# A convolution module on one core: gated tiles left in PSUM, tap products moved last, squares summed by TensorE

## What is computed

```
def conformer_conv_module(u, w_pw1, b_pw1, dw_w, dw_b, ln_g, ln_b, w_pw2, b_pw2):
    h = u @ w_pw1 + b_pw1
    a, g = jnp.split(h, 2, axis=-1)
    h = a * jax.nn.sigmoid(g)
    h = causal_depthwise_conv(h, dw_w, dw_b)      # 31 taps per channel
    h = jax.nn.silu(layernorm(h, ln_g, ln_b))     # mean and variance over the 1024 channels
    return h @ w_pw2 + b_pw2
```

## Time and profile before

| | |
|---|---|
| time, median of 3 runs | 2702.26 us (2699.66 to 2703.58) |
| the profiled execution, its own time | 2701.71 us |
| its span in the profile | 2699.7 us |
| TensorE busy, share of the span | 95% |
| VectorE, ScalarE, GpSimd busy | 50%, 34%, 39% |
| TensorE's mean granted clock | 0.968 of full |
| 40 slices, the 15th to 17th: TensorE busy tenths | 9, 6, 9 |

### The profile page before, as it was taken

The page is one execution under the profiler, slowest core; times in us unless marked ns, Lnnn a source line. Parts: engine busy times, 40 slices in busy tenths (PEclk is TensorE's granted clock), DMA queues, the critical chain, the costliest instruction groups (busy, mean ns, idle before and its releaser), DMA issues.

```text
span 2699.7 us, 29217 instructions
## 1 busy us (share of the span) xinstructions
PE 2570.2 (95%) x11811; PEld 2096.0 (78%) x11811; DVE 1359.8 (50%) x2012; ACT 927.1 (34%) x1539; POOL 1057.5 (39%) x486
## 2 busy tenths in 40 slices
PE   8989999899999996999999899998999999999999
PEld 6778878788888775878888688886766667788887
DVE  6665566565554788474444652224255554422222
ACT  3434334222223284322222232223355543222221
POOL 4333343544444311544444444443222224554443
PEclk9989999899999997999999899999999999999999
DMA  4111221355542200354432232232111112233232
GB/s 147 47 55 62 64 76 50 123 173 164 164 155 95 77 32 8 102 172 161 159 118 94 72 99 97 94 101 78 55 55 47 40 54 86 86 95 100 94 101 86
DMA packets 70982, 252.55 MB, mean 94 GB/s; under 512 B 8000, under 2 KB 8512, under 8 KB 70848
## 3 DMA queue, kind: packets, MB, share of 16 engines
q1 hardware_dynamic: 58752, 210.27, 23.9%
q10 hardware_dynamic: 12096, 40.42, 4.5%
HBM read 248.56 MB, written 2.10 MB: 93 GB/s over the span
## 4 chain that ended last, share of the span: by engine, by line
PE 82%; DVE 13%; ACT 3%; issue 1%; ACTq 0%; DVEq 0%
PE ps L485 24%; PE ps L487 23%; PE ps L486 23%; DVE arena L1359 3%; DVE tmpm L1359 2%; PE ps L501 2%; PE ps L562 1%; PE ps L628 1%; DVE XL L1368 1%; PE ps L702 1%; PE ps L703 1%; PE ps L704 1%; DVE arena L1630 1%; PE ps L524 1%; PE ps L531 1%
## 5 line engine op out<-in xcount | busy, mean ns | idle before, releaser
L2043 POOL TENSOR_TENSOR WL<-raw,WH 128x1024 fp32r<-128x1024 f32 x391 | 953.4, 2442 | 1264.6 <-ACT WH L871 1257.8
L485 PE MATMUL ps<-XH,WH 128*128 128x512 f32 x3160 | 1253.8, 397 | 50.9 <-DVE XL L1359 12.9
L486 PE MATMUL ps<-XL,WH 128*128 128x512 f32 x3160 | 1239.6, 392 | 0.0
L487 PE MATMUL ps<-XH,WL 128*128 128x512 f32 x3160 | 1239.4, 392 | 0.0
L485 PEld LDWEIGHTS ps<-XH,WH 128*128 128x128 f32 x3160 | 600.4, 190 | 187.2 <-issue 24.9
L487 PEld LDWEIGHTS ps<-XH,WL 128*128 128x128 f32 x3160 | 599.0, 190 | 127.3
L486 PEld LDWEIGHTS ps<-XL,WH 128*128 128x128 f32 x3160 | 600.1, 190 | 124.2 <-issue 1.8
L871 ACT ACTIVATE WH<-raw 128x1024 fp32r<-128x1024 f32 x306 | 321.6, 1056 | 682.0 <-PE ps L487 500.2
L1359 DVE SCALAR_TENSOR_TENSOR arena<-arena,ps 128x512 f32<-128x512 f32 x88 | 60.4, 687 | 329.9 <-ACT arena L1072 296.3
L2041 POOL CAST WH<-raw 128x1024 fp32r<-128x1024 f32 x85 | 95.3, 1121 | 279.3 <-PE ps L487 256.1
L1359 DVE SCALAR_TENSOR_TENSOR tmpm<-arena,tmpm 128x512 f32<-128x512 f32 x44 | 83.4, 1895 | 152.1 <-ACT arena L1067 152.1
(11 more groups left out here) (246 smaller groups left out, 2047.4 us busy)
## 6 DMA issues: line engine op xcount, KB each, us to landing
raw<-in_w SPq DMA_DIRECT2D x394, 512.0 KB, 3.7
arena<-in_w_mod ACTq DMA_DIRECT2D x72, 512.0 KB, 4.0
o_out<-h SPq DMA_DIRECT2D x8, 256.0 KB, 2.0
h<-in_x ACTq DMA_DIRECT2D x4, 256.0 KB, 6.9
h<-in_x SPq DMA_DIRECT2D x4, 256.0 KB, 7.3
raw<-in_w SPq DMA_DIRECT2D x2, 256.0 KB, 4.2
arena<-in_c ACTq DMA_DIRECT2D x1, 512.0 KB, 5.4
vec<-in_vec ACTq DMA_DIRECT2D x1, 295.5 KB, 10.3
```

Source lines behind the costliest of these rows:

```text
L485: e.matmul(b, wh, XH[:, x, :], start=i == 0, stop=False)
L486: e.matmul(b, wh, XL[:, x, :], start=False, stop=False)
L487: p = e.matmul(b, wl, XH[:, x, :], start=False, stop=i == len(slots) - 1)
L2043: e.tensor_tensor(lo, x, hi.bitcast(F32), SUB).then_inc(*did(("split", c)))
```

## The change

Six things, all in `conformer()`:

1. Tiles 0 to 2 (`IN_PSUM = 3`) are gated in place in their PSUM bank (5, 6 and 7, `XB`; all the rest of the projection uses the five banks `CB`), and their chains read PSUM. The bank is free when the chain is done. Since no zero padding lies ahead of a tile in PSUM, a step of tap k works on the last 512 - (30 - k) columns only; the steps of the other tiles are cut in the same way.
2. The affine half of the sigmoid moves from VectorE to ScalarE (a second activation behind the tanh).
3. All projections stand ahead of all tap products on TensorE; the numbers of chain steps between the gate instructions change (`more`).
4. The last taps are split, `taps(7, 0, 8)`, the spread of the half mean, `taps(7, 8)`.
5. The squares are summed by TensorE, tile by tile, in PSUM; GpSimd's `squares()` is gone.
6. `centre` and the multiplication by 1/sd read the spread values from PSUM; ScalarE writes its tanh to PSUM; the affine form is made by VectorE (a tensor-scalar into `tmp`).

```
+        IN_PSUM = 3
...
+                CB, XB = (0, 1, 2, 3, 4), (5, 6, 7)
                 for i in range(2, NT):
-                    linear([("pw", 0, 8 + i)], [pw1(8 + i)], X8, x_at, ALL)
-                    linear([("pw", 0, i)], [pw1(i)], X8, x_at, ALL)
-                    if i >= 6:
-                        taps(i - 3)
-                taps(5)
-                taps(6)
-                b = bank(("mean", 0), ALL)
+                    linear([("pw", 0, 8 + i)], [pw1(8 + i)], X8, x_at, CB)
+                    linear([("pw", 0, i)], [pw1(i)], X8, x_at, XB if i < IN_PSUM else CB)
+                for i in range(3, 7):
+                    taps(i)
+                b = bank(("mean", 0), XB)
...
-                taps(7)
+                taps(7, 0, 8)
                 w.wait_ge(*at("mean", 0))
-                spread(("mw", 0), small("mean", 0), ALL)
...
+                spread(("mw", 0), small("mean", 0), XB)
+                taps(7, 8)
+                mean, var = bank(("mean", 1), XB), bank(("var", 0), XB)
+                for i in range(NT):
+                    if i >= 4:
+                        w.wait_ge(*at("cen", i))
+                        p = token_sums(mean, cv[i], one, i == 4, i == NT - 1)
...
+                    w.wait_ge(*at("csq", i))
+                    token_sums(var, tmp[i % 4], one, i == 0, i == NT - 1).then_inc(
...
-                    A(g, g, ACT.Tanh, bias=cols(hb, i), scale=0.5).then_inc(*did(("cgt", i)))
+                    A(g, g, ACT.Tanh, bias=cols(hb, i), scale=0.5).then_inc(*did())
+                    w.wait_ge(s_act, did.n)
+                    A(g, g, ACT.Identity, bias=half_col, scale=0.5).then_inc(*did(("cgt", i)))
...
+                    x = ps("pw", 0, i) if i < IN_PSUM else xp[i][:, K - 1:K - 1 + T]
...
+                        late = K - 1 - k
+                        d = STT(cv[i][:, late:T], x[:, 0:T - late], V("dw_w", 8 * k + i), cv[i][:, late:T], MUL, ADD)
...
-                    if i > 1:
-                        more(10)
+                    more(2 if i > 1 else 0)
...
-                    TS(g, g, 0.5, 0.5, MUL, ADD).then_inc(*did())
...
+                    more((0, 7, 9, 1, 1, 1, 1, 1)[i])
                     if TAPS[i]:
...
+                        more(8)
...
-                    TT(cv[i], cv[i], rs[1], SUB).then_inc(*did(("cen", i)))
+                    TT(cv[i], cv[i], ps("mw", 0), SUB).then_inc(*did(("cen", i), *((("free", "mw", 0),) if i == NT - 1 else ())))
...
-                        TT(cv[i], cv[i], r, MUL).then_inc(*did(("cn", i)))
+                        TT(cv[i], cv[i], ps("vw", 0), MUL).then_inc(*did(("cn", i), *((("free", "vw", 0),) if i == NT - 1 else ())))
+                        own()
+                        w.wait_ge(*at("sum", "var", 0))
+                        TS(zi[i % 4], cv[i], cols(hg, i), cols(hlb, i), MUL, ADD).then_inc(*did(("zi", i)))
...
-            def squares():
```

More of the change, by code:

```diff
@@ L476, in linear @@
             def linear(keys, tiles, slots, ready, of, between=None):
-                bs = [bank(k, of) for k in keys]
+                bs = [bank(k, o) for k, o in zip(keys, of if isinstance(of[0], tuple) else [of] * len(keys))]
                 for i, x in enumerate(slots):
@@ L691, in pw1, with taps @@
                     return column("cv_w_pw1", 0, c)
-                def taps(i):
-                    b = bank(("tap", i), ALL)
+                def taps(i, k0=0, k1=K):
+                    if k0 == 0:
+                        tap_bank[i] = bank(("tap", i), CB)
+                    b = tap_bank[i]
                     a0 = by_pe.index(i) * W
                     w.wait_ge(*at("xp_lo", i))
-                    for k in range(TAPS[i]):
+                    for k in range(k0, min(k1, TAPS[i])):
                         n = sum(TAPS[:i]) + k
@@ L722, in conformer @@
                 p.then_inc(*did(("sum", "mean", 0)))
-                taps(7)
+                taps(7, 0, 8)
                 w.wait_ge(*at("mean", 0))
-                spread(("mw", 0), small("mean", 0), ALL)
[L726 to L735, removed]
+                spread(("mw", 0), small("mean", 0), XB)
[5 more added lines that the diff above has]
+                        p = token_sums(mean, cv[i], one, i == 4, i == NT - 1)
+                        if i == NT - 1:
+                            p.then_inc(*did(("sum", "mean", 1)))
+                    w.wait_ge(*at("csq", i))
+                    token_sums(var, tmp[i % 4], one, i == 0, i == NT - 1).then_inc(
+                        *did(("vs", i), *((("sum", "var", 0),) if i == NT - 1 else ())))
                 w.wait_ge(*at("mean", 1))
-                spread(("mw", 1), small("mean", 1), ALL)
+                spread(("mw", 1), small("mean", 1), CB)
                 w.wait_ge(*at("var"))
-                spread(("vw", 0), small("var"), ALL)
+                for n in range(3):
+                    bank(("t", n), XB)
+                spread(("vw", 0), small("var"), CB)
                 def y_at(i):
@@ L1159, in conformer, with diagonals @@
                 widen(rs[0], ("s2", "w"), ("r", "s2"))
-                def taps(i):
-                    for k in range(TAPS[i]):
+                def diagonals():
+                    for i, k in tap_list:
                         n = sum(TAPS[:i]) + k
@@ L1169, in taps @@
                         A(gl, ident, ACT.Copy, scale=wlo[:, 8 * k + i:8 * k + i + 1]).then_inc(*did(("diag", i, k)))
+                        yield
+                diagonal = diagonals()
                 for i in range(NT):
                     round_weights("pw", 0, i)
-                    if i >= 6:
-                        taps(i - 3)
                     g = cgl[i % 3]
@@ L1183, in conformer @@
                         A(fh[:, a0:a0 + K - 1 + T], xp[i][:, 0:K - 1 + T], ACT.Copy).then_inc(*did(("xp_hi", i)))
[L1184 to L1187, removed]
+                    if i == 5:
+                        for _ in diags:
+                            next(diagonal)
+                for _ in diagonal:
+                    pass
                 sqrt_table()
@@ L1204, in conformer @@
                     if i < NT:
-                        t = tmp[i % 2]
                         w.wait_ge(*at("cn", i))
[L1207 to L1213, removed]
+                        if i >= 3:
+                            w.wait_ge(*at("cy", i - 3))
+                        A(ps("t", i % 3), cv[i], ACT.Tanh, bias=cols(hlb, i), scale=cols(hg, i)).then_inc(*did(("cyt", i)))
                     if i:
@@ L1785, in conformer @@
                 TS(hg, Vs("ln_g", 0, 8), 0.5, None, MUL)
-                TS(hlb, Vs("ln_b", 0, 8), 0.5, None, MUL).then_inc(*did(("hb",)))
-                for a in xp:
-                    e.memset(a[:, 0:K - 1], 0.0).then_inc(*did())
+                TS(hlb, Vs("ln_b", 0, 8), 0.5, None, MUL)
+                e.memset(half_col, 0.5).then_inc(*did(("hb",)))
+                for i in by_pe:
+                    e.memset(xp[i][:, 0:K - 1], 0.0).then_inc(*did())
                 own()
@@ L1800, in chain @@
                         w.wait_ge(s_dve, n)
-                        d = STT(cv[i], xp[i][:, k:k + T], V("dw_w", 8 * k + i), cv[i], MUL, ADD)
-                        d.then_inc(*did(*((("cv", i),) if k == K - 2 and not TAPS[i] else ())))
+                        late = K - 1 - k
+                        d = STT(cv[i][:, late:T], x[:, 0:T - late], V("dw_w", 8 * k + i), cv[i][:, late:T], MUL, ADD)
+                        d.then_inc(*did(*((("cv", i), ("free", "pw", 0, i)) if k == K - 2 and i < IN_PSUM else ())))
                         n = did.n
@@ L1889, in conformer @@
                 less_mean(1)
-                w.wait_ge(*at("r", "cv"))
+                zi = tmp
+                w.wait_ge(*at("sum", "vw", 0))
                 for i in range(NT + 2):
@@ L2020, in pool_program @@
             did = steps.counter("pool")
-            def squares():
-                for i in range(1, NT - 1):
-                    w.wait_ge(*at("csq", i))
-                    if i == 1:
-                        w.wait_ge(*at("csq", 0))
-                    else:
-                        w.wait_ge(*at("csum", i - 1))
-                    e.tensor_tensor(csq, csq, tmp[i % 2], ADD).then_inc(*did(("csum", i)))
             for c in range(HEAD, CHUNKS):
```

48 lines of the change are left out of this document (27 added, 21 removed).

## The result

| | before | after |
|---|---|---|
| median of 4 runs | 2702.92 us (2699.66 to 2704.43) | 2669.88 us (2669.81 to 2670.08) |
| ratio, 95% interval | | 0.9879 (0.9862 to 0.9897) |
| profiled execution, own time | 2701.71 us | 2669.86 us |
| its span | 2699.7 us | 2668.0 us |
| mean granted clock | 0.968 | 0.974 |

The change makes the kernel 33.0 us faster; 2684.5 was forecast, with 2677.5 to 2692 as its range. The sign and the mechanism in the module came as forecast, the size did not: 14.6 us are missing from the sum.

What follows compares the result with a forecast made beforehand. TensorE, busy 95%, bounds the kernel; in the convolution module VectorE's gated tiles and half-mean-to-norm work do. 10.6 + 0.6 + 3.1 + 6.2 - 2.4 + 0.4 - 0.7 = 17.8 takes 2701.71 to 2683.9, as median 2684.5; range 2677.5 to 2692.

Steps and rivals of the forecast that it cites:

- the last of the sum: Behind the convolution module: second projection and feed-forward stay bound by TensorE, their banks read long before; no gain or loss.
- nothing changed behind it but the shift: Sign of being right: behind the second projection's first matmul, at 1059.5, the kernel only moves in time.
- Gated tiles: First projection and taps: PSUM steps at 0.67 us keep VectorE under TensorE's 10.89 a tile; gain 10.6.
- rivals 3 and 4: Late gates: PSUM steps at 0.95 us, 2691.8, chance 0.06; the same place at 1.3 us, 2711.1, chance 0.02.
- Half mean: Sums of four tiles behind the taps: VectorE waits 18 us, reads the mean at 1012.1; 0.6 more gain.
- To the first centred tile: From the half mean on: the wait of 3.11 goes, the spread standing behind only eight taps; gain 3.1.
- Centred tiles: VectorE's centring of the tiles: 13.9 us instead of 20.1 without GpSimd's sum of squares; gain 6.2.
- Rival 5: Last VectorE stretch bound by its own chain, not GpSimd: the 6.2 don't come; 2690.7, chance 0.06.
- The sums of squares: TensorE behind the taps: twelve sums instead of six, four at full clock and eight at half; loss 2.4.
- Rival 1: TensorE keeps full clock through the sums of squares: 5.8 better, 2678.7, chance 0.12.
- rival 2: Half clock from the first sum and splits that meet the norm: 3.7 + 1.2 worse, 2689.4, chance 0.11.
- Norm and first low part: Square sum to second projection: gain 0.4 up to the first product by 1/sd, then loss 0.7.

Runs made afterwards that it cites:

- e1: The kernel before with only the round robin over all eight banks moved on by three ahead of the attention mixer: 2690.91 us, ratio 0.9953.
- e3: The changed kernel with the round robin put back, the spread 1/rms of the mixer's norm in bank 2 as before: 2683.30 us, ratio 0.9926.
- e8: The changed kernel run once more without any edit, as yardstick for the repeats: 2669.79 us, ratio 0.9873.
- e4: The changed kernel with tiles 0 to 2 gated into SBUF and their chains reading SBUF: 2693.57 us, ratio 0.9964.
- e10: The changed kernel with the squares added up by GpSimd again instead of summed by TensorE, second run: 2674.02 us, ratio 0.9889.
- e11: The changed kernel with twelve taps of tile 3 moved from TensorE to VectorE (TAPS[3] = 2), second run: 2666.03 us, ratio 0.9858.
- e7: The changed kernel with twelve taps of tile 3 moved from TensorE to VectorE (TAPS[3] = 2), first run: 2662.28 us, ratio 0.9848.

## Why the prediction missed

The step that failed is the last of the sum: "second projection and feed-forward are bound by TensorE as before; the banks asked for there were read long before", and with it "nothing changed behind it but the shift". For the second projection and the feed-forwards that is true. It was never looked at for the mixer, 730 us further on: the wait of 10.6 for a bank stood in the trace of before, the change alters how many banks `conformer()` takes from ALL, and by that whose bank it is. Both facts could be read in advance, though neither is in the rows: the reach of an edit was taken to end with the function it edits. It was 12.7 us by e1, 13.4 by e3: 9.0 and 7.6 at the mixer's entry, the rest behind it, for the most part in the clock, whose cause stays open. The rest of the miss, 1 to 2 us by these medians, lies in the module, where the traces have 2.4 more than forecast up to the second projection.

The module's own steps. Each row is the gain so far, summed up to that point of the module, in us (1.19 taken off the times after):

| up to | forecast | measured | |
|---|---|---|---|
| sums of the half mean start | 10.6 | 12.4 | 1019.00 - (1007.79 - 1.19) |
| half mean read | 11.2 | 11.9 | 1023.27 - (1012.59 - 1.19) |
| first tile centred | 14.3 | 15.1 | 1039.86 - (1025.92 - 1.19) |
| last tile centred | 20.5 | 21.4 | 1059.25 - (1039.04 - 1.19) |
| square sum read | 18.1 | 20.8 | 1065.38 - (1045.82 - 1.19) |
| first product by 1/sd | 18.5 | 21.2 | 1069.56 - (1049.56 - 1.19) |
| first matmul of the second projection | 17.8 | 20.2 | 1077.28 - (1058.23 - 1.19) |
| end of the module | 17.8 | 20.35 | |

In e8 the gain up to the second projection is 20.1 too; behind that its lower clock lasts longer (0.50 up to 1063 and 0.82 up to 1068, where after has 0.69 and 1.00), and its module is 1.6 longer than that of after.

- *Gated tiles*: right. A step on PSUM takes 725 ns in the median over the shorter rows, 750 at most (0.65 start to start, where 0.67 was taken), TensorE waits for no bank and no diagonal. Late gates and the slower kernel (rivals 3 and 4) are out. What did the work is the place of the source: e4 takes only that away and loses 15 to 16 us of the module.
- *Half mean*: right. The forecast wait of 18 is 19.81. The clock fell within the sums there (4.77 us for four tiles, where 3.72), which took back 1.1 of the 1.8 by which they started ahead of the forecast.
- *To the first centred tile*: right, 3.2 for 3.1. VectorE's wait of 3.11 for the copied half mean is gone (the row at 1025.92 has none). No run puts the split of tile 7's taps or the copy back alone, so their shares are not shown.
- *Centred tiles*: 6.3 for 6.2, but the near agreement is partly luck. The forecast gave all of it to GpSimd's adds; e10 shows 4.7 for them. Rival 5 (none of it comes) is out.
- *The sums of squares*: the loss of 2.4 was 0.6. Five tiles' sums came at full clock where four were taken (1029.38 to 1033.76), the sixth took 1.58 start to start, and a tile at half clock costs 1.71 start to start, not the 1.86 of its duration: neighbours overlap. Rival 1 (full clock throughout) and rival 2 (half from the first) are both out. "TensorE: Matmul & The Clock Gate" of the Trainium skill, section "Why this matters for your kernels", asks, against a drop in mid-kernel, only that TensorE have no idle gaps between bursts of matmuls. By that rule all twelve would have run at full clock. The trace disagrees: the sums follow each other without a gap, and from 1035.34 on a tile takes 1.71 instead of 0.88.
- *Norm and first low part*: 0.4 as forecast; the split met one instruction, the row at 1050.27 (1.85 us, where the same takes 0.55 later), so 1.3 for 1.0. (Two terms of the forecast don't add up to the tenth: 12 x 0.60 + 1.0 is 8.2, not 8.4, and twelve taps behind 1020.3 end at 1028.7, not 1028.5. Neither matters here.)

With the collision put back (e3), the changed kernel came to 2683.3, near the 2684.5 of the forecast. This too is partly luck: its module gained 1 us more than forecast and the feed-forward behind it 3.4, while the mixer's next stretch was 1.7 longer than before.

## What to carry to other kernels

When a shared counter (a round robin of banks, a ring of buffers) hands out places, an edit that changes how often it is asked changes every later place: list the later users that were waiting on it, and work out the new places before summing. A broadcast left in PSUM holds its bank until its last reader, so give it a bank that the next matmuls don't ask for; TensorE starting behind the last reader of a row group, instead of behind the first input, is how it shows. If VectorE and GpSimd run beside each other, a long chain is best fed from PSUM, even at a few ns more an instruction; and once a rebalancing leaves VectorE idle, move work to it at once.

## What the runs showed of the hardware that was not expected

The same instructions, at the same place, take one of a few lengths from one kernel to the next, because the clock granted to TensorE there falls or does not. The stretch from 1916 to 1954 of before is 37.00, 38.52, or 40.2 to 41.5 us. It starts with short matmuls and pauses. The first 12 us of it in the changed kernel (length; busy us (instructions) of PE, PE's weight loads, VectorE, ScalarE, GpSimd; granted clock; DMA share; GB/s):

```profile
1887.86:1891.86 4.00, 2.23 (x25) 1.82 (x24) 1.71 (x4) 2.73 (x6) 0.00 (x0) 1.00 0.21 82
1891.86:1895.86 4.00, 3.68 (x17) 2.53 (x18) 2.38 (x4) 1.14 (x3) 0.00 (x0) 1.00 0.00 0
1895.86:1899.86 4.00, 4.00 (x19) 3.31 (x18) 3.79 (x4) 0.34 (x1) 2.86 (x1) 1.00 0.00 0
```

And in e11:

```profile
1878.68:1882.68 4.00, 2.24 (x25) 1.82 (x24) 1.71 (x4) 2.73 (x6) 0.00 (x0) 0.94 0.10 38
1882.68:1886.68 4.00, 3.68 (x6) 1.62 (x6) 1.53 (x3) 0.27 (x1) 0.00 (x0) 0.50 0.01 4
1886.68:1890.68 4.00, 4.00 (x15) 3.52 (x14) 2.56 (x5) 1.21 (x2) 1.07 (x1) 0.50 0.00 0
```

In both TensorE is busy 2.2, 3.68 and 4.00 of the 4 us; in one it gets 2.4 GHz throughout, in the other 1.2 GHz for the last 8 us and somewhat beyond, and 4.5 us are lost. No run here shows what decides it.

The feed-forward behind the module also took 357.7 or 354.3, even in two executions of the same program (after and e8), but not by the clock. TensorE waits there for VectorE to add a tile to `h`, in after and in e8:

```profile
PE ps L486 <- DVE h L1406: 3.3, 1, 3.3
PE ps L486 <- DVE h L1406: 0.6, 1, 0.6
```

VectorE comes to that addition at 1186.24 in after and at 1186.36 in e8. TensorE is 3 us earlier in after, and what it was ahead is lost in the wait. The kernel before has the wait of 3.3 as well. So a gain in one stretch can vanish at the next wait for another engine.

For a change worth a few us, then, the stretch that it touches has to be compared, in more than one execution. e7 and e11 are one kernel, and their medians differ by 3.8 us (2662.28 and 2666.03), as much as the four times of e7 spread (3.8; those of e11 spread by 2.0).
